# Attention stage of an encoder layer: the values product of a pair over two steps, its halves transposed on TensorE and added by VectorE, the value operand in two homes, the four head groups written out

## What is computed

```
def token_mixer(x, w_in, q_norm_g, k_norm_g, w_pool, pool_scale, w_out):
    proj = x @ w_in
    q, k, v, u = split(proj)                  # 8 query heads, 2 key/value heads of 64; u: 512 columns
    q = axial_rope(rms_norm(q, q_norm_g), tabs)
    k = axial_rope(rms_norm(k, k_norm_g), tabs)
    attn = softmax(q @ k.T / 8) @ v           # 4 query heads share one key/value head
    pool = pool_mixer(u, w_pool, pool_scale)
    return concatenate([attn, pool], axis=-1) @ w_out
x = layer_norm(ALPHA * x + token_mixer(...))
x = layer_norm(ALPHA * x + expert_choice_ffn(x, ...))   # 16 experts, 128 tokens of each sequence per expert
```

## Time and profile before

| what | value |
|---|---|
| device time, median of three runs | 3181.15 us (3179.3 to 3182.24) |
| device time of the profiled execution | 3181.95 us |
| its span, first to last instruction | 3180.1 us |
| mean granted clock of TensorE | 0.987 |
| TensorE busy | 3084.6 us (97%) |
| VectorE busy | 1806.6 us (57%) |
| ScalarE busy | 1443.0 us (45%) |
| transposes of the probabilities (L782), 1024 | 135.2 us |
| values products (L793), 1024 | 130.4 + 125.2 us |
| score products (L711, L712), 512 | 108.9 + 101.3 us |
| products that add the halves (L804), 256 | 38.7 us |

### The profile page before, as it was taken

The page is one execution under the profiler, slowest core; times in us unless marked ns, Lnnn a source line. Parts: engine busy times, 40 slices in busy tenths (PEclk is TensorE's granted clock), DMA queues, the critical chain, the costliest instruction groups (busy, mean ns, idle before and its releaser), DMA issues.

```text
span 3180.1 us, 43744 instructions
## 1 busy us (share of the span) xinstructions
PE 3084.6 (97%) x15912; PEld 2609.8 (82%) x15912; DVE 1806.6 (57%) x1887; ACT 1443.0 (45%) x1801; POOL 420.4 (13%) x373
## 2 busy tenths in 40 slices
PE   8999999999968999999999999999999999999997
PEld 7998989978856888888888888888888888888885
DVE  6546877866664454545545455454545545455587
ACT  3226878861123444444444444444444444444464
POOL 2554232401130000010100000000000000001000
PEclk9999999999978999999999999999999999999998
DMA  6331101113244566565656656566565656656585
GB/s 212 125 109 52 34 9 31 37 64 120 113 168 157 181 217 202 193 212 179 216 186 209 211 181 215 181 214 203 192 212 180 213 189 207 212 182 213 182 291 199
DMA packets 371531, 532.71 MB, mean 168 GB/s; under 512 B 36720, under 2 KB 311920, under 8 KB 371440
## 3 DMA queue, kind: packets, MB, share of 16 engines
q1 hardware_dynamic: 356560, 488.50, 45.6%
q0 software_dynamic: 10656, 38.80, 4.7%
q10 hardware_dynamic: 4224, 4.19, 0.4%
HBM read 470.62 MB, written 60.82 MB: 167 GB/s over the span
## 4 chain that ended last, share of the span: by engine, by line
PE 88%; issue 4%; DVE 2%; POOLq 2%; POOL 1%; DMA 1%; ACT 1%; DVEq 0%; ACTq 0%; SPq 0%
PE ps_gu L971 44%; PE ps_y L1009 22%; PE ps_o L859 6%; PE ps_pv L793 4%; PE ps_t L782 3%; PE ps_s L711 2%; PE ps_s L712 2%; PE ps_x L985 2%; PE ps_m L804 1%; POOLq L1779 1%; PE ps_x L948 1%; POOLq L1771 1%; PE ps_l L876 1%; POOL qkv L1785 1%; POOL rot L1774 0%
## 5 line engine op out<-in xcount | busy, mean ns | idle before, releaser
L1611 DVE TENSOR_TENSOR w_l<-w_raw,w_h 128x2048 fp32r<-128x2048 f32 x380 | 871.1, 2292 | 777.8 <-ACT w_h L1264 777.8
L1264 ACT ACTIVATE w_h<-w_raw 128x2048 fp32r<-128x2048 f32 x384 | 734.2, 1912 | 587.3 <-PE ps_gu L971 371.8
L971 PE MATMUL ps_gu<-w_h,x_h 128*128 128x512 f32 x2048 | 808.8, 395 | 0.0
L971 PE MATMUL ps_gu<-w_h,x_l 128*128 128x512 f32 x2048 | 799.0, 390 | 0.0
L971 PE MATMUL ps_gu<-w_l,x_h 128*128 128x512 f32 x2048 | 798.1, 390 | 0.0
L971 PEld LDWEIGHTS ps_gu<-w_h,x_l 128*128 128x128 f32 x2048 | 384.7, 188 | 82.0
L971 PEld LDWEIGHTS ps_gu<-w_l,x_h 128*128 128x128 f32 x2048 | 385.2, 188 | 76.7
L971 PEld LDWEIGHTS ps_gu<-w_h,x_h 128*128 128x128 f32 x2048 | 385.0, 188 | 76.8
L1009 PE MATMUL ps_y<-w_h,hh 128*128 128x512 f32 x1024 | 323.7, 397 | 0.0
L1009 PE MATMUL ps_y<-w_l,hh 128*128 128x512 f32 x1024 | 317.2, 391 | 0.0
L1009 PE MATMUL ps_y<-w_h,hl 128*128 128x512 f32 x1024 | 316.5, 390 | 0.0
(11 more groups left out here) (276 smaller groups left out, 3989.9 us busy)
## 6 DMA issues: line engine op xcount, KB each, us to landing
w_raw<-in_w_gate SPq DMA_DIRECT2D x256, 512.0 KB, 3.6
w_raw<-in_w_up SPq DMA_DIRECT2D x256, 512.0 KB, 4.7
w_raw<-in_w_down SPq DMA_DIRECT2D x128, 1024.0 KB, 4.9
xin<-in_x SPq DMA_DIRECT2D x16, 512.0 KB, 5.6
xln_d<-xln SPq DMA_DIRECT2D x16, 512.0 KB, 5.2
res<-xln_d SPq DMA_DIRECT2D x16, 512.0 KB, 3.3
h_d<-hid SPq DMA_DIRECT2D x16, 512.0 KB, 2.6
acc_d<-acc SPq DMA_DIRECT2D x16, 512.0 KB, 2.6
```

Source lines behind the costliest of these rows:

```text
L971: last = nc.tensor.matmul(out_gu, a[:, k, tok], w[:, kk, :], start=k == 0 and q == 0, stop=k == KD - 1 and q == 2)
L1264: nc.scalar.activation(w_h[:, c % RING, :], w_raw[:, c % RING, :], ACT.Copy).then_inc(w_hi, 1)
L1611: nc.vector.tensor_tensor(w_l[:, c % RING, :], w_raw[:, c % RING, :], w_h[:, c % RING, :].bitcast(f32), ALU.subtract).then_inc(w_lo, 1)
```

## The change

- `values(b, part)` makes eight of the 16 products in each of two steps: part 0 in the even step after the pair, part 1 in the odd step after that. The copy `o_hl` moves to the beginning of ScalarE's even step.
- `add_halves` is two plain transposes with the full identity. Both halves arrive in `ps_m` untouched; VectorE multiplies the low half by the reciprocal into a new tile `at_rest`, waits for that (`drain`), and with two fused instructions (one for each block of 128 queries) multiplies the high half and adds. `ident2` and its two loads are gone, so `b_const` counts to 48 and not to 80.
- `add_halves` moves to even steps (ahead of `values`), `back` to odd steps. The queries' turns move from steps 3 and 5 to steps 4 and 5; those of the keys stay at 7, 9, 23 and 25. Four steps follow slot 3, not three.
- `v_hl` has two homes, `v_even` and `v_odd`, by the slot's parity (the second lies in what was the unused `b_gap`). ScalarE's `v_hi_copy` moves to the beginning of step 1.
- Stage B is written out for all four slots on SP, TensorE, ScalarE and VectorE; GpSimd's was so before.

```diff
-        B_GAP = 1544
+        B_GAP = 1544 + 64 - GT * P
+        v_odd = sb("v_odd", [P, GT, P], f32r)
-        v_hl = sb("v_hl", [P, GT, P], f32r)
+        v_even = sb("v_even", [P, GT, P], f32r)
+        v_hl = (v_even, v_odd)
+        at_rest = sb("at_rest", [P, 2, HD])
...
-        q_turn_at = {3: 0, 5: 1}
+        q_turn_at = {4: 0, 5: 1}
...
-            pv = t // 2 - 1 if t % 2 == 0 else None
-            add = (t - 3) // 2 if t % 2 == 1 else None
-            back = (t - 4) // 2 if t % 2 == 0 else None
+            pv = (t - 2) // 2
+            add = (t - 4) // 2 if t % 2 == 0 else None
+            back = (t - 5) // 2 if t % 2 == 1 else None
...
-            for t in range(NSTEP + (3 if last else 0)):
+            for t in range(NSTEP + (4 if last else 0)):
...
# TensorE
-                def values(b):
-                    pe.wait_ge(pt_lo, 2 * (NSTEP * s + 2 * b + 2))
-                    if b == 0:
-                        pe.wait_ge(v_split, s + 1)
-                    if not (first and b == 0):
-                        pe.wait_ge(o_ready, NQB * s + b)
-                    for k in range(GT):
+                def values(b, part):
+                    if part == 0:
+                        pe.wait_ge(pt_lo, 2 * (NSTEP * s + 2 * b + 2))
+                        if b == 0:
+                            pe.wait_ge(v_split, s + 1)
+                        if not (first and b == 0):
+                            pe.wait_ge(o_ready, NQB * s + b)
+                    for k in range(GT // 2 * part, GT // 2 * (part + 1)):
...
-                    last.then_inc(pv_done, 1)
+                    if part == 1:
+                        last.then_inc(pv_done, 1)
...
                     for c in range(2):
-                        last = nc.tensor.matmul(ps_m[:, c, 0:HD], o_hl[:, b % 2, c * P:(c + 1) * P], ident2[:, :],
-                                                start=True, stop=True)
+                        last = nc.tensor.transpose(ps_m[:, c, :], o_hl[:, b % 2, c * P:(c + 1) * P], ident[:, :])
...
-                    if pv is not None:
-                        values(pv)
                     if add is not None:
                         add_halves(add)
+                    if pv is not None:
+                        values(pv, t % 2)
                     if bk is not None:
                         back(bk)
...
-            steps(pe, SLOTS, stage_b)
+            for s in range(SLOTS):
+                stage_b(s, s == 0, s == SLOTS - 1)
...
# ScalarE
-                if not first:
-                    act.wait_ge(pv_done, NQB * s)
-                nc.scalar.activation(v_hl[:, :, 0:HD], v_raw[:, :, :], ACT.Copy).then_inc(v_hi, 1)
+                if s >= 2:
+                    act.wait_ge(pv_done, NQB * (s - 1))
+                nc.scalar.activation(v_hl[s % 2][:, :, 0:HD], v_raw[:, :, :], ACT.Copy).then_inc(v_hi, 1)
...
+                    _, add, bk = after_step(t, first)
+                    if add is not None:
+                        act.wait_ge(pv_done, NQB * s + add + 1)
+                        nc.scalar.activation(o_hl[:, add % 2, :], ps_pv[:, 0:QB], ACT.Copy).then_inc(o_ready, 1)
+                    if t == 1 and not first:
+                        v_hi_copy(s, False)
                     if t < NSTEP:
                         for what in before_step(t, last_s):
                             from_m(turn_no(s, last_s, what), what, there)
...
-                    if pv is not None:
-                        act.wait_ge(pv_done, NQB * s + pv + 1)
-                        nc.scalar.activation(o_hl[:, pv % 2, :], ps_pv[:, 0:QB], ACT.Copy).then_inc(o_ready, 1)
-                        if pv == -1:
-                            v_hi_copy(s, False)
...
# VectorE
-                        nc.vector.tensor_tensor(at_tok[:, i:i + 2, (h % 2) * HD:(h % 2 + 1) * HD], ps_m[:, 0:2, 0:HD],
-                                                rinv[:, j:j + 2].unsqueeze(2).to_broadcast([P, 2, HD]),
-                                                ALU.mult).then_inc(m_free, 1)
+                        nc.vector.tensor_tensor(at_rest[:, :, :], ps_m[:, 0:2, HD:P],
+                                                rinv[:, j:j + 2].unsqueeze(2).to_broadcast([P, 2, HD]), ALU.mult)
+                        dve.drain()
+                        for c in range(2):
+                            last = nc.vector.scalar_tensor_tensor(at_tok[:, i + c, (h % 2) * HD:(h % 2 + 1) * HD],
+                                                                  ps_m[:, c, 0:HD], rinv[:, j + c:j + c + 1],
+                                                                  at_rest[:, c, :], ALU.mult, ALU.add)
+                        last.then_inc(m_free, 1)
```

More of the change, by code:

```diff
@@ L163, in encoder_layer @@
         win_b = sb("win_b", [P, SEQ + 2 * PAD])
-        ident2 = sb("ident2", [P, HD])
         edge_t = sb("edge_t", [P, NW, 2, PAD])
@@ L384, in encoder_layer @@
         first_turns = [("Q", 0, 0), ("Q", 0, 1)]
[L385 removed]
+        TURN0 = len(first_turns) - 4
         def turn_no(s, last, what):
@@ L495, in _ @@
             stage_end(sp, 1)
-            for dst, src in ((ident2[0:HD, :], eye[0:HD, 0:HD]), (ident2[HD:P, :], eye[0:HD, 0:HD]),
-                             (edge_t[:, :, :, :], pool_edge.rearrange("p (w s n) -> p w s n", w=NW, s=2)),
+            for dst, src in ((edge_t[:, :, :, :], pool_edge.rearrange("p (w s n) -> p w s n", w=NW, s=2)),
                              (wp_sb[:, :, :], w_pool.rearrange("w c d -> c w d")),
@@ L783, in transposes @@
                         last.then_inc(t_done, 1)
[L785 to L791 removed]
+                def values(b, part):
[6 more added lines that the diff above has]
+                    for k in range(GT // 2 * part, GT // 2 * (part + 1)):
                         for n, pt in enumerate((pt_h, pt_l)):
[L793 removed]
+                            last = nc.tensor.matmul(ps_pv[:, 0:QB], v_hl[(s + b // NQB) % 2][:, k, :], pt[:, b % 2, k, :],
                                                     start=k == 0 and n == 0, stop=k == GT - 1 and n == 1)
[L795 removed]
+                    if part == 1:
+                        last.then_inc(pv_done, 1)
                 def add_halves(b):
                     pe.wait_ge(o_ready, NQB * s + b + 1)
[L800 to L801 removed]
                     m_turn(("add", b))
                     for c in range(2):
[L804 to L805 removed]
+                        last = nc.tensor.transpose(ps_m[:, c, :], o_hl[:, b % 2, c * P:(c + 1) * P], ident[:, :])
                     last.then_inc(m_full, 1)
@@ L814, in back @@
                     last.then_inc(m_full, 1)
-                for t in range(NSTEP + (3 if last_s else 0)):
+                for t in range(NSTEP + (4 if last_s else 0)):
                     if t < NSTEP:
@@ L826, in stage_b @@
                     pv, add, bk = after_step(t, first)
-                    if pv is not None:
-                        values(pv)
                     if add is not None:
                         add_halves(add)
+                    if pv is not None:
+                        values(pv, t % 2)
                     if bk is not None:
                         back(bk)
-            steps(pe, SLOTS, stage_b)
+            for s in range(SLOTS):
+                stage_b(s, s == 0, s == SLOTS - 1)
+            pe.wait_ge(b_const, 48)
             for n in range(GROUPS * NW):
@@ L1180, in stage_b @@
                             exp(s + 1, t + 2 - NSTEP, False)
-                    pv, add, bk = after_step(t, first)
                     if last_s and t == NSTEP:
@@ L1195, in stage_b @@
                                              ps_m[:, 0:2, :].rearrange("p c t -> p (c t)"), ACT.Copy).then_inc(m_free, 1)
-            steps(act, SLOTS, stage_b)
+            for s in range(SLOTS):
+                stage_b(s, s == 0, s == SLOTS - 1)
             def mix_hi(i, sl, start):
@@ L1510, in stage_b @@
                         dve.wait_ge(m_full, turn_no(s, last_s, ("add", add)) + 1)
-                        nc.vector.tensor_tensor(at_tok[:, i:i + 2, (h % 2) * HD:(h % 2 + 1) * HD], ps_m[:, 0:2, 0:HD],
-                                                rinv[:, j:j + 2].unsqueeze(2).to_broadcast([P, 2, HD]),
-                                                ALU.mult).then_inc(m_free, 1)
-            steps(dve, SLOTS, stage_b)
+                        nc.vector.tensor_tensor(at_rest[:, :, :], ps_m[:, 0:2, HD:P],
[6 more added lines that the diff above has]
+                        last.then_inc(m_free, 1)
+            for s in range(SLOTS):
+                stage_b(s, s == 0, s == SLOTS - 1)
             def mix_lo(i, sl):
```

9 lines of the change are left out of this document (4 added, 5 removed).

## The result

The changed kernel takes 3185.3 us (median of 20 runs, 3183.59 to 3188.45), the kernel before 3180.76 beside it (20 runs, 3177.99 to 3182.42): ratio 1.0015, interval 1.0009 to 1.0022. Forecast were 0.07% less; measured are 0.15% more. The time lies in the range given, the sign is the other one. The profiled execution has a span of 3184.0 us, 3.9 more than before.

What follows compares the result with a forecast made beforehand. TensorE's issue was taken to bound stage B. Terms -14.7 - 4.5 - 4.9 - 1.7 + 16.8 + 3.6 + 2.3 + 1.0 = -2.1 us gave 3179.85 from the profiled 3181.95, a median forecast of 3179.0 us, range 3170 to 3187.

Steps and rivals of the forecast that it cites:

- adds, 64 pairs: Stage B on TensorE: two transposes replace four half products, a pair of steps takes 5.78 in place of 6.01 us: -14.7 us.
- turns beside an add: Stage B: 42 steps lose 0.13 us to an add waiting for ScalarE's copy; after, 15 lose about 0.07: -4.5 us.
- loop: Stage B's branch back: writing out the slots removes 3.5 us of empty TensorE and 1.4 of half clock: -4.9 us.
- value operand: Step 2 of the three slots after the first: 0.58 us each lost to `v_hl`'s single home goes: -1.7 us.
- turns behind an add: TensorE waits for VectorE to empty `ps_m`, 0.66 us at 12 keys' turns and 0.59 at 15 queries' turns: +16.8 us.
- turns behind `back`: First queries' turn in step 4 waits for ScalarE's copy, 0.36 us seven times, more at three slot starts: +3.6 us.
- tail with its clock: End of slot 3: `wo_lo_sub` ahead of pair 14's add delays pooling, +2.3 us, and half clock there, +1.0 us.
- VectorE empties in time: Rival on `ps_m`: fused instructions at 0.16 us give 3172.5 us, no turn waiting 3158.6; chances 0.20 and 0.07.
- the price of 0.28 us for a fused instruction: VectorE's add: each fused instruction on 64 columns from PSUM takes 0.28 us, bounds 0.16 and 0.29.
- VectorE becomes the bound: Rival in stage B's pairs: costlier fused instructions exceed VectorE's 0.11 us margin, past 3187.5 us, up to 3208.4; chance 0.13.
- Written-out slots: Rival in stage B: written-out code waits for instructions as the loop did, the 4.9 us do not come, 3183.9 us; chance 0.08.

Runs made afterwards that it cites:

- the run with the loop alone: The kernel before, with stage B's four slots written out on SP, TensorE, ScalarE and VectorE and nothing else changed: 3176.51 us, ratio 0.9986.
- the shorter: The changed kernel with VectorE doing one product in place of three instructions, the low half left out of the output: 3166.36 us, ratio 0.9950.
- the longer: The changed kernel with VectorE's two fused instructions of each add done twice, a drain between: 3216.39 us, ratio 1.0111.
- the old add: The changed kernel with the add in its former form, four products with `ident2` and one product of VectorE: 3174.2 us, ratio 0.9976.
- The run with the other order: The changed kernel with a turn's two waits swapped, so the wait for the bank stands on the first weight load: 3183.5 us, ratio 1.0006.
- the last version: The changed kernel with turns moved to other steps, the bank's wait last and VectorE's weight subtractions behind the last add: 3160.08 us, ratio 0.9935.

## Why the prediction was wrong

The mechanisms were right in the main, the sum was not. Point by point, in us of the span; "measured" is worked out from steps of the traces or the run named.

| term | forecast | measured | from |
|---|---|---|---|
| adds, 64 pairs | -14.7 | -18.6 | 6.01 - 5.72; 0.23 of it the add, 0.06 the order |
| turns beside an add | -4.5 | -3.1 | 42 x 0.11 less 15 adds that are 0.10 late |
| loop | -4.9 | -4.1 | the run with the loop alone; 4.8 at the branch, 0.7 lost elsewhere |
| value operand | -1.7 | about -1.7 | step 2 without its wait, 2.97; not run alone |
| turns behind an add | +16.8 | +21.1 | 12 x 0.83 + 15 x 0.72, and 0.35 at one |
| turns behind `back` | +3.6 | +4.3 | steps of 4.05 (3) and 3.77 (4) against 3.28 |
| tail with its clock | +3.3 | +4.7 | 15.34 against 10.63 |
| sum | -2.1 | +2.6 | span: +3.9 |

Of the difference 1.3 us are spread over other steps and not assigned. The 0.11 of a turn beside an add is from the run with the loop alone: the odd step takes 2.40 in place of 2.26, but the even step behind it 3.72 in place of 3.75. The prediction had read the first of these only (0.13).

**The step that failed** is "So it waits 0.66 us at 12 keys' turns, and 0.59 at 15 queries' turns": 16.8 us that measured 21.1. Its cause was named rightly, as the shorter, the longer and the old add show, and the emptying's end (3.61) was exact. What failed is the way from there to TensorE. I took 0.05 us from a row of the loop, where the wait stood on the weight load; written out, the wait for the bank became an instruction of its own ahead of the load, and the first product starts 0.14 us behind VectorE. The run with the other order brought the 0.05 us and T + 3.66 back. The other part was not in the sum at all: behind the wait the turn takes 0.35 to 0.38 in place of 0.30, its first load starting only 0.03 us ahead of its first product or together with it. And TensorE comes to the wait at T + 2.97, not 3.00.

**The tail** was short by 1.4 us. The pooling products came 3.5 us later against step 31 (684.77 - 674.32 = 10.45, before 682.00 - 675.09 = 6.91), not 2.3. The subtractions alone were priced rightly: the run that moves them takes 2.3 of it back (8.11). The other 1.2 stay in the new order without them; step 31 now also holds half of the values of pair 14, which stood in step 30 before. The half clock took 1.2 (4.89 us from there to VectorE's emptying, before 3.72), near the 1.0 given; that this came out is luck, since the run with the other order of waits lost 2.7 there with the same start. **The adds** were under-estimated by 3.9 us, which hid part of the other errors; that the time stayed in the range is owed to this.

**The rivals.** That VectorE empties in time did not happen; the price of 0.28 us for a fused instruction was right (280 ns median of 128), and so was the 0.20 us from the start of the first to that of the second. The Trainium skill, "VectorE: DVE Perf Modes", TRN2 errata, would have it at an estimated 0.19; the duration in the trace does not agree, the distance of the two starts nearly does. That VectorE becomes the bound did not happen either, but it was a little nearer than the prediction had it: VectorE's pair is 5.64, as summed up, TensorE's came out at 5.72 in place of 5.78, and the margin is 0.08 us, not 0.11. One fused pair more showed the stretch at once. Written-out slots did not wait for instructions: at the branch 4.8 us came, nearly what the row said, against the estimated 0.1 of the Trainium skill, "Advanced Engine Details and Errata", Control Flow Timing.

Two things I did not weigh. The gain of the add was counted as TensorE's alone; in the old order VectorE's longer add takes all of it back. (The prediction puts VectorE's idle 0.93 us into the odd step; it lies mostly at the end of the long even step, 650.80 to 651.73, with the odd step beginning at 651.53.) And the largest term, these waits, is not part of the change's idea: it hangs on which steps the turns stand in. In other steps they all but vanish, and the change, with the subtractions of the tail moved as well, is 0.65% faster than before.

## What to carry to other kernels

When work moves from the bounding engine to another one, price it at every place where the bounding engine hands a shared buffer over, not only by the sum of busy times: in the new order 0.55 us more on VectorE cost nothing in 37 plain pairs and 0.55 us in each of 27 others. Look which other step could hold the handover, before giving the edit up. And take the latency of a wait from a row where the wait has the same form: on the load itself, or on an instruction of its own.

## What the runs showed of the hardware

- A semaphore wait of TensorE on the weight load let it start 0.05 us after the releasing instruction's end, one on an instruction of its own (51 ns) 0.11; which of two waits stands on the load follows from their order in the program.
- The clock in the tail: in the run with the subtractions moved and in the last version TensorE's rows from step 31 to the pooling products stand at the same distances (last add at 6.47, last `back` at 7.84, pooling at 8.11 us), yet the granted clock fell to 0.50 in the one and stayed at 1.00 in the other. VectorE's first emptying came 13.53 and 11.83 us after step 31: 1.7 us for 3.4 us of half clock. In the run with the other order of waits the half clock lasted 6.8 us, where in the changed kernel, with pooling at the same place, it lasted 3.4. What decided is open; the tail's rows alone do not.
- VectorE's fused instruction with a scalar per row took 280 ns for 64 columns from PSUM; the second of two in a row started 0.20 us behind the first.
